# A two-block transformer in one launch: where the memory's key and value projections run, and how long GpSimd's subtraction instructions are

## The reference, cut to what matters

```python
h = first_block(x, ...)            # qkv, indexer and gating projections, sparse attention, spatial gate, router, 32 experts
mem_n = rmsnorm(mem, mem_norm_g)   # mem: 256 x 1024
for layer in range(2):
    u = rmsnorm(h, norm_g[layer, 0])
    mem_kv = mem_n @ w_mem_kv[layer]                  # 1024 x 1024: keys (512) and values (512) of 4 heads
    y = mixer[layer](u, mem_kv, ...)                  # 0: windowed attention with rope + attention to memory
                                                      # 1: gated linear recurrence (HGRN2) + attention to memory
    h = h + rmsnorm(y, norm_g[layer, 1])
    f = conv_ffn(rmsnorm(h, norm_g[layer, 2]), ...)   # 1024 -> 2 x 2816, conv over time, gelu, -> 1024
    h = h + rmsnorm(f, norm_g[layer, 3])
```

## Time and profile before

| | us |
|---|---|
| median of 3 runs | 1517.81 (1516.28 to 1519.84) |
| the profiled execution | 1517.31, of which the span of the core's instructions is 1515.6 |
| PE busy | 1280.2 (84%) |
| POOL busy | 782.3 (52%), of which L732 773.2 |
| DVE, ACT busy | 601.1 (40%), 632.7 (42%) |
| DMA | 275 MB, mean 181 GB/s |

### The profile page before, as it was taken

The page is one execution under the profiler, slowest core; times in us unless marked ns, Lnnn a source line. Parts: engine busy times, 40 slices in busy tenths (PEclk is TensorE's granted clock), DMA queues, the critical chain, the costliest instruction groups (busy, mean ns, idle before and its releaser), DMA issues.

```text
span 1515.6 us, 19422 instructions
## 1 busy us (share of the span) xinstructions
PE 1280.2 (84%) x7815; PEld 1063.8 (70%) x7815; DVE 601.1 (40%) x1010; ACT 632.7 (42%) x1042; POOL 782.3 (52%) x347
## 2 busy tenths in 40 slices
PE   5789998885877877996889799997898668699997
PEld 4668877765433533785667799986797557599986
DVE  3937763443111111308661332203318984322311
ACT  3434443532111111642454455444557524455542
POOL 3939985430000000896104688877476621588884
PEclk9889999996999999998899899998999889899999
DMA  6534545253799999564003366444433420555552
GB/s 215 177 128 150 184 167 190 75 206 127 315 410 409 410 410 407 187 222 153 28 1 110 113 190 199 154 168 165 137 142 111 137 100 1 167 168 168 196 192 70
DMA packets 138330, 275.00 MB, mean 181 GB/s; under 512 B 7380, under 2 KB 53772, under 8 KB 138252
## 3 DMA queue, kind: packets, MB, share of 16 engines
q1 hardware_dynamic: 137980, 272.87, 50.2%
q10 hardware_dynamic: 272, 1.05, 0.2%
HBM read 272.85 MB, written 1.05 MB: 181 GB/s over the span
## 4 chain that ended last, share of the span: by engine, by line
PE 65%; DVE 15%; DMA 6%; ACT 6%; POOL 3%; issue 2%; SPq 0%; DVEq 0%; ACTq 0%
PE lin_ps L801 8%; PE lin_ps L802 8%; PE lin_ps L803 8%; PE lin_ps L821 8%; PE lin_ps L823 8%; PE lin_ps L824 8%; POOL w_low L732 3%; DMA ring<-in_w_expert_in 3%; PE lin_ps L1021 3%; PE sc_ps L1035 3%; ACT w_high L1255 2%; PE lin_ps L1049 1%; PE tr_ps L1058 1%; DVE work L2003 1%; DVE work L2001 1%
## 5 line engine op out<-in xcount | busy, mean ns | idle before, releaser
L732 POOL TENSOR_TENSOR w_low<-ring,w_high 128x1024 fp32r<-128x1024 f32 (+1 forms) x320 | 773.2, 2452 | 716.2 <-ACT w_high L1255 716.0
L1255 ACT ACTIVATE w_high<-ring 128x1024 fp32r<-128x1024 f32 (+1 forms) x320 | 311.7, 1040 | 123.9 <-PE lin_ps L803 78.6
L821 PE MATMUL lin_ps<-x_high,w_high 128*128 128x256 f32 x960 | 274.9, 286 | 2.6 <-DVE cross_low L593 2.6
L823 PE MATMUL lin_ps<-x_high,w_low 128*128 128x256 f32 x960 | 274.1, 286 | 0.0
L824 PE MATMUL lin_ps<-x_low,w_high 128*128 128x256 f32 x736 | 209.7, 285 | 0.0
L801 PE MATMUL lin_ps<-w_high,x_high 128*128 128x512 f32 (+1 forms) x464 | 184.3, 397 | 21.9 <-POOL w_low L732 20.8
L821 PEld LDWEIGHTS lin_ps<-x_high,w_high 128*128 128x128 f32 x960 | 187.2, 195 | 2.9 <-DVE cross_low L593 2.8
L823 PEld LDWEIGHTS lin_ps<-x_high,w_low 128*128 128x128 f32 x960 | 186.9, 195 | 0.0
L802 PE MATMUL lin_ps<-w_low,x_high 128*128 128x512 f32 (+1 forms) x464 | 182.3, 393 | 0.0
L803 PE MATMUL lin_ps<-w_high,x_low 128*128 128x512 f32 (+1 forms) x400 | 155.1, 388 | 0.0
L824 PEld LDWEIGHTS lin_ps<-x_low,w_high 128*128 128x128 f32 x736 | 142.8, 194 | 0.0
(11 more groups left out here) (351 smaller groups left out, 2083.1 us busy)
## 6 DMA issues: line engine op xcount, KB each, us to landing
ring<-in_w_expert_in SPq DMA_DIRECT2D x32, 2048.0 KB, 16.1
ring<-in_ffn_w_in SPq DMA_DIRECT2D x44, 1024.0 KB, 7.7
ring<-in_w_expert_out SPq DMA_DIRECT2D x16, 2048.0 KB, 19.6
ring<-in_w_in SPq DMA_DIRECT2D x15, 2048.0 KB, 7.8
ring<-in_b_w_in SPq DMA_DIRECT2D x11, 2048.0 KB, 8.0
ring<-in_ffn_w_out SPq DMA_DIRECT2D x8, 2048.0 KB, 7.9
ring<-in_w_mem_kv SPq DMA_DIRECT2D x4, 2048.0 KB, 10.6
ring<-in_a_w_in SPq DMA_DIRECT2D x4, 2048.0 KB, 8.0
```

Source lines behind the costliest of these rows:

```text
L732: pool.tensor_tensor(w_low[:, slot, 0:words], raw, w_high[:, slot, 0:words].bitcast(F32), ALU.subtract).then_inc(low_made, 1)
L821: pe.matmul(out, wh[:, j, at], high(k), start=(k == 0 and f < 2), stop=False, skip_group_check=True)
L823: pe.matmul(out, wl[:, j, at], high(k), start=False, stop=False, skip_group_check=True)
L1255: act.activation(w_high[:, slot, 0:words], raw, ACT.Copy).then_inc(high_made, 1)
```

## The change

It does two things.

**The memory's blocks move.** The pieces and PE's blocks kv00, kv01, kv10, kv11 no longer stand together. kv00 stays first, with u0's turn at its sixth k; kv01 comes behind a3 and takes over the turns of q2 and k2 (at its sixth k), so a3 has none; kv10 comes behind o01, ahead of the wait for f0's norm; kv11 behind fo01, ahead of the wait for u1's norm. ACT's copies and splits move with them: kv10 is copied behind f0's high parts, kv11 behind u1's, and ahead of those high parts ACT splits two units more than the block's own piece (`split_units(... + 2)`). In `work` the parts of the memory now lie in buffers 6 and 9, where they live until kv11, the feed-forward's low part moves to buffer 7, and keys and values of layer 1 go to what is free by then.

**POOL's instructions get shorter.** A unit is subtracted in instructions of 128x256 (`SHORT`), four for a full unit, with the semaphore on the last, for all pieces but those of the feed-forwards (names that begin with "f").

```diff
+SHORT = 256
@@ order of the pieces
-    for layer in range(LAYERS):
-        for j in range(2):
-            weight_block(f"kv{layer}{j}", [(io["w_mem_kv_2"][layer], j * NB, NB)], NB)
+    memory_block(0, 0)
     for layer in range(LAYERS):
         if layer == 0:
             for j in range(4):
                 weight_block(f"a{j}", [(io["a_w_in_2"][0], j * NB, NB)], NB)
+            memory_block(0, 1)
...
             weight_block(f"o{layer}{j}", ...)
+        if layer == 0:
+            memory_block(1, 0)
...
             weight_block(f"fo{layer}{j}", ...)
+        if layer == 0:
+            memory_block(1, 1)
@@ POOL, split_to
-                        pool.tensor_tensor(w_low[:, slot, 0:words], raw, w_high[:, slot, 0:words].bitcast(F32),
-                                           ALU.subtract).then_inc(low_made, 1)
+                        step = words if p in whole_units else SHORT
+                        for at in range(0, words, step):
+                            cut = slice(at, min(at + step, words))
+                            ins = pool.tensor_tensor(w_low[:, slot, cut], raw[:, cut], w_high[:, slot, cut].bitcast(F32),
+                                                     ALU.subtract)
+                        ins.then_inc(low_made, 1)
@@ PE
-            linear_turned("kv00", *parts(mem_high, mem_low))
-            linear("kv01", *parts(mem_high, mem_low))
-            linear_turned("kv10", *parts(mem_high, mem_low))
-            linear("kv11", *parts(mem_high, mem_low),
-                   ready=amid(2, lambda: pe.wait_ge(normed, 5), lambda: turn_split("u0", 8, scaled)))
+            from_mem = parts(mem_high, mem_low)
+            linear_turned("kv00", *from_mem,
+                          ready=amid(5, lambda: pe.wait_ge(normed, 5), lambda: turn_split("u0", 8, scaled)))
...
-            linear_turned("a3", *parts(x_high, x_low5),
+            linear_turned("a3", *parts(x_high, x_low5))
+            linear("kv01", *from_mem,
                    ready=amid(5, lambda: pe.wait_ge(roped, 6), lambda: turn("q2", 8, both(q2_roped)),
                               lambda: turn("k2", 4, both(k2_twice))))
...
+            linear_turned("kv10", *from_mem)
             pe.wait_ge(normed, 7)
             feed_forward(0)
...
+            linear("kv11", *from_mem)
             pe.wait_ge(normed, 9)
@@ ACT, feed_forward
                 take_high(act, f"f{layer}", 8, x_high, f"f{layer}")
+                if layer == 0:
+                    copy_turned("kv10", four(km_T[1]), then_split=False)
@@ ACT, order
-            for layer in range(LAYERS):
-                copy_turned(f"kv{layer}0", four(km_T[layer]), then_split=layer == 0)
-                if layer == 1:
-                    take_high(act, "u0", 8, x_high, "u0")
-                    split_to(piece("kv10") + 2)
-                copy_block(f"kv{layer}1", v_mem[layer])
+            take_high(act, "u0", 8, x_high, "u0")
+            copy_turned("kv00", four(km_T[0]))
...
+            copy_turned("a3", four(xqT))
             tr_take(act, 0, "q2", 8, plain(q2_T))
-            copy_turned("a3", four(xqT))
+            copy_block("kv01", v_mem[0])
...
             norm_root(6, h, 3)
+            split_units(sum(units[piece("kv10")]) + 2)
             feed_forward(0)
...
             norm_root(8, h, 4)
+            split_units(sum(units[piece("kv11")]) + 2)
             take_high(act, "u1", 8, x_high, "u1")
-            split_to(piece("fo01") + 2)
+            copy_block("kv11", v_mem[1])
```

More of the change, by code:

```diff
@@ L160, in program, with memory_block @@
     first_block_pieces = len(pieces)
-    for layer in range(LAYERS):
-        for j in range(2):
-            weight_block(f"kv{layer}{j}", [(io["w_mem_kv_2"][layer], j * NB, NB)], NB)
+    def memory_block(layer, j):
+        weight_block(f"kv{layer}{j}", [(io["w_mem_kv_2"][layer], j * NB, NB)], NB)
+    memory_block(0, 0)
     for layer in range(LAYERS):
@@ L248, in program @@
         xT = sb("xT", [P, KC, SEQ])
-        x_low4, x_low5, x_low6, x_low7 = (overlay(f"x_low{i}", 2048 * i, [P, KC, SEQ]) for i in (4, 5, 6, 7))
-        mem_high, mem_low = overlay("mem_high", 8 * 2048, [P, KC, SEQ]), overlay("mem_low", 3 * 2048, [P, KC, SEQ])
-        cat_high, cat_low = overlay("cat_high", 4 * 2048, [P, 12, SEQ]), overlay("cat_low", 6 * 2048, [P, 12, SEQ])
+        x_low4, x_low5, x_low7 = (overlay(f"x_low{i}", 2048 * i, [P, KC, SEQ]) for i in (4, 5, 7))
+        mem_high, mem_low = overlay("mem_high", 6 * 2048, [P, KC, SEQ]), overlay("mem_low", 9 * 2048, [P, KC, SEQ])
+        cat_high, cat_low = overlay("cat_high", 4 * 2048, [P, 12, SEQ]), overlay("cat_low", 7 * 2048, [P, 12, SEQ])
         hidden_high = overlay("hidden_high", 0, [P, FC, SEQ])
@@ L450, in program @@
         mem_raw = tok(buf(6))
-        scaled_mem = tok(buf(9))
-        km_T = [feat(buf(7, 1024)), feat(buf(9, 1024))]
-        v_mem = [tok(buf(7, 1024, 1024)), tok(buf(9, 1024, 1024))]
+        scaled_mem = tok(buf(8))
+        km_T = [feat(buf(7, 1024)), feat(buf(5, 1024, 1024))]
+        v_mem = [tok(buf(7, 1024, 1024)), tok(buf(7, 1024))]
         q2_raw, q2_roped, q2_T = tok(buf(0)), tok(buf(1)), feat(buf(8))
@@ L723, in _ @@
             pool.memset(eps[:], EPS).then_inc(pool_made, 1)
+            whole_units = {n for name, (_, used, _) in blocks.items() if name.startswith("f") for n, _, _ in used}
             split = [0]
@@ L1068, in feed_forward @@
                 for j in range(FB):
-                    linear_turned(f"ff{layer}_{j}", *parts(x_high, x_low6), ready=made(f"f{layer}") if j == 0 else None)
+                    linear_turned(f"ff{layer}_{j}", *parts(x_high, x_low7), ready=made(f"f{layer}") if j == 0 else None)
                 for j in range(2):
@@ L1912, in feed_forward @@
                 norm_rows(i, h, scaled_f)
-                take_low(dve, f"f{layer}", 8, x_high, x_low6, f"f{layer}")
+                take_low(dve, f"f{layer}", 8, x_high, x_low7, f"f{layer}")
                 for j in range(FB):
```

## The result

The changed kernel takes 1536.6 us (median of four runs, 1531.4 to 1537.7), the kernel before 1518.8 in the runs beside it. The ratio is 1.0109 (95% interval 1.0078 to 1.0140). The forecast was 1488 us, with a range of 1475 to 1503.

What follows compares the result with a forecast made beforehand. PE was taken as the bound, with gaps waiting on DVE's norms and ropes, slowed by POOL. Terms -1 + 26 - 1 + 7 - 1.5 = 29.5 us off 1517.3 gave 1487.8, 1488 against the median; range 1475 to 1503 (8 in 10).

Steps and rivals of the forecast that it cites:

- first block, to the end of w_out: To 346 us: relief of the queries' rope and the merge, outweighed by POOL's dearer units; 1 us lost.
- kv00 to the attention: Memory blocks and second block's rope: PE's gaps filled, rope wait gone, attention 91 us behind kv00's start; 26 us gained.
- kv10 and kv11 in their gaps: Moved blocks fill PE's waits for norms after o01 and fo01; 1 us lost, at kv10.
- b projections and gated heads: Scans relieved, b3 ending 2 us later, level scores starting 1 us behind it instead of 10; 7 us gained.
- o1 to the second feed-forward: The feed-forward's weights are issued later, behind POOL's slower units of o11's first piece; 1.5 us lost.
- the prices: Costs shared by all parts: 0.70 us per 128x256 subtraction; a DVE instruction meeting POOL about 1.2 us instead of 2.8.
- rival B: Ropes and scans: relief fails, DVE waits out POOL's four short instructions as one long; 1513 us, chance 0.07.
- my 121 us for these ten blocks: First block, v0 to gb1: PE's 114 us become 121 behind POOL's slower units, 7 us lost.
- D: Where POOL is the bound, it starves PE: 1530 us at 0.86 us per short instruction; chance 0.04.

Runs made afterwards that it cites:

- d256: The changed kernel, with POOL waiting for its own end once per unit, after every fourth 128x256 subtraction: 1500.0 us, ratio 0.9871.
- b512: The changed kernel with 128x512 subtractions and the turn of u0 after k-step 7 instead of 5: 1486.8 us, ratio 0.9787.
- m1: The changed kernel with whole-unit subtractions (128x1024), so the moved blocks alone: 1504.0 us, ratio 0.9899 to the kernel before.
- w256: The changed kernel, with POOL waiting for its own end after each 128x256 subtraction: 1524.0 us, ratio 1.0034.

## Why the forecast was wrong, step by step

Stretches of the changed kernel against those of before, from the starts of PE's blocks:

| step | forecast | measured | with the wait per unit (`d256`) |
|---|---|---|---|
| first block, to the end of w_out | -1 | -11.4 | -10.5 |
| kv00 to the attention | +26 | -3.8 | +31.6 |
| kv10 and kv11 in their gaps | -1 | -5.5 | -6.8 |
| b projections and gated heads | +7 | +7.4 | +6.0 |
| o1 to the second feed-forward | -1.5 | -3.9 | -2.1 |

(+ is a gain in us. What is missing to the difference of the spans, -18.2 and +17.5, is 1 us or less in the stretches between.)

**The step that failed** is one clause of the prices, the wait of DVE: "A DVE instruction that meets POOL then waits 0.5 us instead of 2.1", and behind it, against rival B, "the two engines change over at every boundary seen". What was seen were boundaries with a short past: in the kernel before POOL is faster per unit (2.36 us), so it catches up with ACT and pauses, and its records show no more than 8 subtractions in a row without a pause or a DVE instruction let in between. The change broke that twice. A unit is four instructions, so 13 or 14 come together after three and a half units; and a unit costs 2.78 us, so POOL falls behind and seldom pauses. The two rows of POOL above are series of 32 and of 80. DVE needn't do anything new to be locked out.

**Memory blocks and rope.** Of the 29.8 us between forecast and measurement two waits hold 28.7: u0's norm (18.2 us of idle PE where 7.5 was forecast) and the rope (20.0 where 2 was). Both are lock-outs, and with the wait per unit the term came out, 5.6 better than forecast. The mechanism of this term, the filling of PE's gaps and the relief of the rope, was right; it rests on the failed clause.

**First block.** Three errors. The queries' rope was relieved (v0 starts 4.2 us earlier, forecast 4.5). From v0 to the end of gb1 11.1 us were lost, not 7, since my 121 us for these ten blocks were 125.1. PE waits there 3.5 us for `w_low` and 3.6 at the turn for ACT (1.3 before), and between these waits it is itself slower: busy for 117.6 us instead of 112.0, at a granted clock of 0.98, 0.79 and 0.91 ahead of, in and behind the turn where it was 1.00 throughout. The sum had no term for that. And the merge, for which I had 1.5 us of gain, waits out a run of POOL (L1788, 15.72 us) and costs 3.9 more than before. The lock-outs alone don't sink this block: in `d256` there are none and it loses as much, since each wait makes a unit dearer (v0 to the end of gb1 is 127.3 us there). 512 columns help here (`b512` starts kv00 6 us before the old kernel): a unit is 2.5 us instead of 2.8.

**kv10 and kv11.** Forecast free, and so they are with whole units: in `m1` the turns behind them come 12.5 and 11.4 us after the block before, as without them (12.6 and 11.2). With short ones they stick out by 4.1 and 2.6 us. I had kept "up to 3" each for POOL's being late: the value taken was wrong, and kv10 passed the bound as well.

**b projections and heads** came out as forecast in the sum, but not in its parts. b3 ended 2.2 us earlier (counted from the end of b0) where 2 later was forecast; PE starts the level scores 1.1 us behind it instead of 10.1, as forecast; and from there to o1 it takes 3.7 us more than before, where nothing was put, since DVE's instructions for the second pair of heads (L2096) now run beside POOL's series: four of them take 3.18 and 3.53 us there, 1.42 where POOL is idle. The first and the last error nearly cancel, which is luck. The scans came when POOL's series had been short (5 us after its last pause at the first of them) and took turns with it.

**o1 and the feed-forward** lost 2.4 more than forecast. ACT starts to split the feed-forward's weights, which it waits for, 35.6 us behind o1's start instead of 31.6. Of these 3.9 us 1.6 come from PE, whose first eight k of o1 take 12.8 us instead of 11.2 though it waits for nothing and POOL is idle. Its granted clock there is 0.50, the 1.2 GHz level, for 3 us, after the pauses between the heads (columns as in the earlier trace rows):

```profile
1276.00:1284.00 8.00, 4.86 (x37) 4.24 (x37) 5.30 (x17) 4.58 (x17) 0.00 (x0) 0.99 0.00 0
1284.00:1287.00 3.00, 3.00 (x8) 2.30 (x7) 0.26 (x1) 0.00 (x0) 0.00 (x0) 0.50 0.02 5
```

In `d256` the same eight k have 1.00 and take 11.2 us, and this step loses 2.1 us.

**Of the rivals** B ("DVE still waits out POOL's four short ones as it did one long") was the nearest, with 0.07. It had the right place and the wrong size: it made the lock-out end with the unit, which gives 1513; that it could last for the run, none of my cases had. The one that ended slower, D, was priced by the length of a short instruction, and that price was right to 0.01 us. The form of the argument was at fault: a rule of arbitration was read off rows of another regime and priced as nearly certain. One reading of the earlier trace rows is also wrong, and nothing hangs on it: PEclk is 9 in the 28th slice, and the lowest slice of PE, the 10th with 5, isn't named.

The Trainium skill, "SBUF — State Buffer", "Who interferes with whom", says that an exclusive lock on a shared port pair is what DVE and GpSimd contend for, held for a whole instruction while the other blocks fully. The trace agrees on who meets whom: reads of PSUM took 0.4 us in the midst of POOL's runs. It doesn't agree on how long: 35.28 us beside instructions of 0.70.

## What to carry to other kernels

Where DVE and POOL both work from SBUF, don't price a meeting by one boundary: count how many instructions POOL issues without a pause, and keep that well under a dozen (12 subtractions and a select were too many in three kernels, 6 subtractions in one trial beside PE), with longer instructions or with a wait for POOL's own end every few. Cutting an engine's work into shorter instructions buys shorter waits for its neighbour only while the engine still pauses; if the cut also makes it the slower one, it hardly does. And a regularity seen in a trace is evidence for the regime of that trace alone: ask which count, rate or backlog the change moves outside it.

## What the hardware showed that I had not expected

- With the other engines idle, a DVE instruction that reads two SBUF operands is let in between two of POOL's while at most 12 subtractions of an undisturbed run are done and, with few exceptions, waits out the run from the 15th on, at every length from 128 to 1024 columns: 35.28 us beside 256 columns, 41.30 beside 1024. `TENSOR_SCALAR` from SBUF to SBUF was caught too (31.95 us). With PE at work it can begin sooner: in one trial with 6 done.
- POOL's wait for its own end, once in 16 instructions, was enough to prevent it; waits already met and raised semaphores weren't. Its price: a 128x256 subtraction and its wait take 0.82 us instead of 0.70 in `w256`, 0.80 instead of 0.68 with the other engines idle.
- A lock-out can end before the run does: in the changed kernel when DVE had waited out 46 and 10 subtractions, in `b512` after 5, in seven trials beside PE's multiplications when 47 of the run were done, and in seven with 128 columns when 46 were. But runs of 64 with 256 columns and idle engines went on past 47 and held DVE to their end. What ends it, and what decides at 13 and 14, stays open.
- A subtraction of POOL takes 0.41, 0.68, 0.95, 1.22, 1.76 and 2.30 us for 128, 256, 384, 512, 768 and 1024 columns: 0.14 us and 2.1 us per 1000 columns. The line through the 144- and the 1024-column rows had given 0.71 for 256.
